# Four buffers for the decode's key pages, two of them placed in the row buffer that the input projection has finished reading

## The chip, the cores and the metric

The kernel runs on one core of a Trainium2 chip. The metric is the device time of one execution in microseconds; lower is better. The core has five engines that run their own instruction streams: TensorE (PE, matrix products), VectorE (DVE), ScalarE (ACT), GpSimd (POOL) and SyncE (SP). In this kernel SP and POOL issue nearly all DMAs in the stage that matters, and the transfers share 16 DMA engines.

## The reference, cut to what matters

One inference step of a two-layer decoder, for 256 prompt tokens and 8 sample (decode) tokens. Each layer projects its normalised input with `w_in` (1024 to 2048 columns) and mixes it in three ways; the part that matters is the attention of the 8 sample tokens over their cached keys and values, 256 positions in two pages of 128:

```python
def diff_attend(q, k, v, q_pos, k_pos, table, lam):
    s = jnp.einsum('bqhmd,bkhmd->bhmqk', q, k) * (DIFF_HEAD_DIM ** -0.5)
    s = s + rel_position_bias(q_pos, k_pos, table)[None, :, None]
    p = jax.nn.softmax(s, axis=-1)
    w = p[:, :, 0] - lam * p[:, :, 1]
    return jnp.einsum('bhqk,bkhe->bqhe', w, v)

k_past = cache_k[page_table, l]     # per sample: 2 pages x 128 positions x 512 numbers
v_past = cache_v[page_table, l]
```

After the mixers come the output projection `w_out` and a mixture of 64 experts (8 of them per token) with one shared expert. Six slices of `w_ada` times the conditioning vectors give the modulation of each layer.

## The kernel before, in words

All is float32. Activations lie transposed, features on the 128 partitions and the 264 tokens along the free axis: `hT` (8 x 264 columns) is the normalised input, `projT` the projected one. Semaphores order the engines by hand; a `Signal` counts per layer, and `by(layer, k)` is the k-th event of that layer. There are two layers, and each has the same stages.

*Projection.* TensorE makes 16 blocks of `w_in` times `hT` (line 1055) and signals `proj_made` after each. The weights come through `wide`, a pair of 2 MB buffers; SP fills them (line 614). A fill is two DMAs of 1 MB. Fill f = 5, the second with `w_ada`, waits for `proj_made` 16, the last block. Fills 6, 7 and 8 wait for the `ada` products 5, 6 and 7 of the layer in turn.

*Decode scores.* POOL loads pages with `load_k` and `load_v` (both through the helper on line 733), two DMAs of 256 KB for one sample. Keys go into `kbuf`, which has two buffers, values into `vbuf`, which has four. Samples 0 and 1 of the keys are loaded before the projection, the values of samples 0 to 3 when the last sine is made; the order on POOL's queue after that is this:

```python
for b in range(4):
    load_v(b)
for b in range(2, NS):
    pool.wait_ge(dec_products.sem, dec_products.by(layer, b - 1))
    load_k(b)
for b in range(4, NS):
    pool.wait_ge(dec_pv.sem, dec_pv.by(layer, b - 3))
    load_v(b)
```

For each sample b, TensorE copies its query row to all partitions (line 1122, into one of two PSUM banks, after the products of sample b - 2). VectorE multiplies it with the two key pages (line 1918, two instructions; the second signals `dec_products`) and sums over the features (line 1921). Between these TensorE has the two GLU products (line 1128, after sample 1) and the sixteen matmuls of `ada` (line 943, after the query of sample 4 and again after that of sample 7), and one turn of a modulation row (line 951). Then it waits for the last sum (`dec_scored`).

*Decode weights and values.* TensorE turns the scores (lines 903, 1140), VectorE and ScalarE make the softmax (lines 1930 to 1937), TensorE spreads the weights (lines 1145, 1146), and the values of samples 0 to 3 are multiplied (line 1153). Their `dec_pv` lets POOL load the values of samples 4 to 7. Behind them on POOL stand the stores of new keys, values and states (line 805).

*After that:* prompt attention with the remaining `ada` products, the output projection (line 1235), routing, the shared expert (line 1289), and then 96 expert steps. An expert step multiplies 64 gathered rows with the gate and up weights (line 1337) and with the down weights (line 1350); POOL gathers the rows into `xg` (line 842), and scatters the results (line 849). `hT` is written again by ScalarE with the squares of the second norm, after the first block of the output projection has been added.

Of the kernel before, what the change touches and what calls it, by code (L numbers as in the profile page):

```python
# [22 lines left out]
ALU = mybir.AluOpType  # L23
# [5 lines left out]
DEPTH = 2  # L29
NP_ = 256  # L30
NS = 8
# [9 lines left out]
PROJ = IN_W // P  # L41
# [5 lines left out]
PAGES = PAST // PAGE  # L47
# [152 lines left out]
def program(nc, a, out):  # L200
    ctx_list = []

    def keep(cm):
        ctx_list.append(cm)
        return cm.__enter__()
# [3 lines left out]
    def sb(name, shape, dt=F32):  # L209
        places[name] = -(-nc.sbuf_base // 32) * 32  # L210
        return keep(nc.sbuf_tensor(name, shape, dt))
# [5 lines left out]
    def sem(name):  # L217
        return keep(nc.semaphore(name))

    def sig(name, per_layer):  # L220
        return Signal(sem(name), per_layer)
# [4 lines left out]
    hT = sb("hT", [P, KD, T])  # L226
# [5 lines left out]
    kbuf = sb("kbuf", [P, 2, PAGES, 512])  # L232
# [50 lines left out]
    ps = keep(nc.psum_tensor("ps", [P, 8, 512], F32))  # L283
# [6 lines left out]
    ident = cst[:, K_ID:K_ID + P]  # L290
    ones = cst[:, K_ONE:K_ONE + P]
    half = cst[:, K_HALF:K_HALF + 2]

    xrows = projT[:, :, :].rearrange("p a b -> p (a b)")[:, 0:4 * D].rearrange("p (a b) -> p a b", a=4)
    skews = scratch[:, 0:HEADS * BUCKET_COLS].rearrange("p (h i) -> p h i", h=HEADS)
# [2 lines left out]
    prod = scratch[:, 0:1024].rearrange("p (g n) -> p g n", g=PAGES)  # L298
# [112 lines left out]
    proj_made = sig("proj_made", PROJ)  # L411
    proj_copied = sig("proj_copied", PROJ)
    rows_made, rows_out = sig("rows_made", 9), sig("rows_out", 9)
    k_loaded = [sig(f"k_loaded{n}", 16 * PAGES * NS // 2) for n in range(2)]
    v_loaded = [sig(f"v_loaded{n}", 16 * PAGES * NS // 4) for n in range(4)]
    q_spread = sig("q_spread", NS)
    dec_products = sig("dec_products", NS)
# [311 lines left out]
    def _(pool):  # L729
        gp = nc.gpsimd  # L730

        def load(sem_, dst, src):
            pool.dma_start(dst, src, allow_slow_non_contiguous=True).then_inc(sem_, 16)  # L733
# [22 lines left out]
        pages = [pool.value_load(pt[0:1, n:n + 1], min_val=0, max_val=kc.shape[0] - 1) for n in range(NS * PAGES)]  # L756
        kcf = kc.rearrange("n l t h d -> (n l) t (h d)")
        vcf = vc.rearrange("n l t h d -> (n l) t (h d)")
        pool.sem_inc(cache_stored, 1)
        for layer in range(DEPTH):  # L760

            def load_k(b):
                for g in range(PAGES):
                    load(k_loaded[b % 2].sem, kbuf[:, b % 2, g, :], kcf[pages[b * PAGES + g] * DEPTH + layer])

            def load_v(b):
                for g in range(PAGES):
                    load(v_loaded[b % 4].sem, vbuf[:, b % 4, g, :], vcf[pages[b * PAGES + g] * DEPTH + layer])
# [4 lines left out]
            for b in range(2):  # L773
                load_k(b)
# [17 lines left out]
            pool.wait_ge(sines_ready.sem, sines_ready.by(layer, 1 + SC // 2))  # L792
            for b in range(4):
                load_v(b)
            for b in range(2, NS):
                pool.wait_ge(dec_products.sem, dec_products.by(layer, b - 1))
                load_k(b)
            for b in range(4, NS):
                pool.wait_ge(dec_pv.sem, dec_pv.by(layer, b - 3))
# [35 lines left out]
            for t in range(3):  # L835
                n = P if t < 2 else NS
# [807 lines left out]
    def _(dve):  # L1644
        v = nc.vector
        ts, tt, stt, cp = v.tensor_scalar, v.tensor_tensor, v.scalar_tensor_tensor, v.tensor_copy
# [4 lines left out]
        for m in range(2):  # L1651
            ins = cp(relbs[:, :, :, m], relb[:, :].unsqueeze(1).to_broadcast([32, NS, HEADS]))
# [165 lines left out]
        for layer in range(DEPTH):  # L1818

            def W(s, k=1):  # L1820
                dve.wait_ge(s.sem, s.by(layer, k))
# [12 lines left out]
            for r in range(2):  # L1834
                for h in range(2):
                    src = ps[:, 6, 256 * r:256 * r + 256].rearrange("p (t k h c) -> p t k h c", t=2, k=4, h=2)[:, :, :, h, :]
                    dst = cT[:, r].rearrange("p t (k h c) -> p t k h c", k=4, h=2)[:, :, :, h, :]
                    for t in range(2):
                        ins = ts(dst[:, t], src[:, t], half[:, h:h + 1], -1.0 if r else 1.0, ALU.mult, ALU.mult)
# [64 lines left out]
            for c in range(2):  # L1904
                ins = stt(yv[:, c, :], projT[:, C_U + c, :], pT[:, R_SD + c:R_SD + c + 1], ps[:, 4 + c, 0:T], ALU.mult, ALU.add)
# [7 lines left out]
                ts(prodm[:, :, :, m], qk[:, :, :], half[:, m:m + 1], None, ALU.mult)  # L1913
            for b in range(NS):
                W(q_spread, b + 1)
                dve.wait_ge(k_loaded[b % 2].sem, k_loaded[b % 2].by(layer, 32 * (b // 2 + 1)))
                for g in range(PAGES):
                    ins = tt(prod[:, g, :], ps[:, 2 + b % 2, :], kbuf[:, b % 2, g, :], ALU.mult)
                ins.then_inc(dec_products.sem, 1)
                W(dec_products, b + 1)  # L1920
                ins = v.tensor_reduce(decS[:, :, 8 * b:8 * b + 8], prod.rearrange("p g (a d) -> p g a d", d=HD), AX.X, ALU.add)
                if b == NS - 1:
                    ins.then_inc(dec_scored.sem, 1)
                else:
                    chain(ins)
                if b == 3:
                    W(glu_gate)
                    tt(mixT[:, 6:8, :], zv, gv, ALU.mult).then_inc(ssm_mixed.sem, 1)
# [12 lines left out]
            for g in range(PAGES):  # L1941
                for b in range(NS):
                    ins = cp(w32[:, g, b, 4 * b:4 * b + 4], ps[:, 7, 32 * g + 4 * b:32 * g + 4 * b + 4])
# [32 lines left out]
            for h in range(HEADS):  # L1976
                ins = cp(oT[:, h, NP_:T], ps[:, 5, 32 * h:32 * h + 32].rearrange("p (b h) -> p h b", h=HEADS)[:, h, :])
# [25 lines left out]
            for c in range(KD):  # L2003
                W(out_made, c + 1)
                g = modT[:, 16 + c, :]
# [26 lines left out]
            for t in range(3):  # L2032
                for g in range(NG):
                    ins = v.max(g8[:, t, g, :], biased[:, t, PG * g:PG * g + PG])
# [4 lines left out]
            for t in range(3):  # L2039
# [3 lines left out]
                ins = tt(pairs2[:, t], other, me, ALU.is_equal)  # L2043
            chain(ins)
            for t in range(3):
                ins = tt(pairs2[:, t], pairs2[:, t], low, ALU.mult)
# [7 lines left out]
            for t in range(3):  # L2054
                ins = v.max(t8[:, t, :], masked[:, t, :])
            chain(ins)
            for t in range(3):
                ins = v.match_replace(masked[:, t, :], t8[:, t, :], masked[:, t, :], 3 * NEG)
# [24 lines left out]
            for t in range(3):  # L2083
                ins = v.max(t8[:, t, :], order[:, t, :])
# [7 lines left out]
            for t in range(3):  # L2092
                n = P if t < 2 else NS
# [71 lines left out]
            for k in range(TOPK):  # L2165
                for t in range(2):
                    W(y_loaded[k // 2], 32)
                    part, g = ypart[t][k // 2][:, k % 2, :], gk[:, t, k:k + 1]
# [52 lines left out]
```

## Time and profile before

| | us |
|---|---|
| median of 3 runs | 1956.47 |
| lowest and highest | 1954.2, 1957.7 |
| the profiled execution's own time | 1957.11 |
| its span | 1955.4 |
| TensorE busy | 1756.3 (90%) |
| VectorE busy | 670.0 (34%) |
| mean granted TensorE clock | 0.923 |

The span is counted from the first to the last instruction of the profiled execution; its own time holds 1.7 us more. A row of a timeline has its start in us, its duration in us, the engine, the source line, what is written and read, the count of instructions merged, and in brackets how long the engine stood idle before it and what released it.

### The profile page before, as it was taken

Reading aid. Unit: us, or ns where it says so; the run is one execution under the profiler, and the core shown is the slowest. Engines: PE = TensorE matmul, PEld = TensorE weight load, DVE = VectorE, ACT = ScalarE, POOL = GpSimd, SP = SyncE. Lnnn points to the kernel's source line nnn. Section 1 sums busy time; section 2 is a strip of 40 time slices with the busy share of each in tenths; the row PEclk is TensorE's granted clock in tenths of the full one; section 3 lists DMA queues with packets and bytes.
Section 4 is the critical chain, followed back from the end, with each engine's and each line's share of the span. In section 5 each row is a group of like instructions: output and inputs, shape, how many; then the busy total and the mean of one; then the engine's idle time right before and its main releaser. Section 6 shows DMA issues by size and latency. Waiting matters only on the chain.

```text
span 1955.4 us, 28143 instructions
## 1 busy us (share of the span) xinstructions
PE 1756.3 (90%) x11215; PEld 1004.8 (51%) x11215; DVE 670.0 (34%) x1678; ACT 341.3 (17%) x765; POOL 692.2 (35%) x754
## 2 busy tenths in 40 slices
PE   6996888999999999999589779788999999999974
PEld 3762466455555555555267337644555555555533
DVE  4773435322112322112469522541122112222216
ACT  3230311111112111111021221211111111111101
POOL 1214102445445455454012140053545445455420
PEclk9897688999999999999879778889999999999996
DMA  9457654998999999999934675579999999999943
GB/s 302 132 167 237 208 194 178 414 379 307 393 407 391 355 367 377 373 372 351 342 106 137 198 242 197 213 297 415 389 372 365 370 347 381 365 357 372 371 170 139
DMA packets 216639, 588.89 MB, mean 301 GB/s; under 512 B 67705, under 2 KB 147277, under 8 KB 162622
## 3 DMA queue, kind: packets, MB, share of 16 engines
q1 hardware_dynamic: 146224, 506.99, 67.9%
q0 software_dynamic: 67232, 79.73, 12.0%
q8 instruction: 90, 1.47, 0.3%
q10 hardware_dynamic: 3054, 0.38, 0.2%
q14 instruction: 39, 0.32, 0.0%
HBM read 775.22 MB, written 56.95 MB: 426 GB/s over the span
## 4 chain that ended last, share of the span: by engine, by line
PE 75%; DVE 8%; DMA 7%; issue 5%; SPq 2%; ACT 1%; another core or an unknown queue 1%; POOL 1%; POOLq 0%; ACTq 0%; DVEq 0%
PE ps L1337 34%; PE ps L1350 15%; PE ps L900 8%; PE ps L1055 4%; DMA xg<-hrows,idx_x 3%; PE ps L1235 3%; PE ps L943 2%; DMA ypart<-yrows_k 2%; PE ps L1289 1%; SPq L618 1%; PE ps L929 1%; DMA vbuf<-in_cache_v 1%; DMA raw<-in_w_ada 1%; PE ps L1266 1%
## 5 line engine op out<-in xcount | busy, mean ns | idle before, releaser
L1337 PE MATMUL ps<-raw,xTs 128*64 128x256 f32 x6144 | 745.4, 394 | 1.4 <-ACT xTs L1595 1.4
L1337 PEld LDWEIGHTS ps<-raw,xTs 128*64 128x64 f32 x6144 | 418.6, 135 | 268.8 <-issue 37.0
L849 POOL DMA_INDIRECT yrows_k<-ytok,idx_y x192 | 195.8, 1020 | 514.4 <-DVE ytok L2020 470.3
L1350 PE MATMUL ps<-dn,scratch 128*64 128x512 f32 x1536 | 363.6, 592 | 1.6 <-DVE scratch L2024 1.5
L2014 DVE TENSOR_TENSOR scratch<-scratch,ps 128x128 f32<-128x128 f32 x192 | 55.2, 288 | 750.6 <-ACT scratch L1617 662.1
L842 POOL DMA_INDIRECT xg<-hrows,idx_x x192 | 197.6, 1029 | 124.7 <-DVE idx_x L2108 66.5
L2020 DVE COPY ytok<-ps 128x512 f32<-128x512 f32 x192 | 132.7, 691 | 154.6 <-PE ps L1350 116.9
L1350 PEld LDWEIGHTS ps<-dn,scratch 128*64 128x64 f32 x1536 | 108.9, 135 | 146.9 <-issue 111.3
L1595 ACT ACTIVATE xTs<-ps 128x512 f32<-128x512 f32 x192 | 114.4, 597 | 382.3 <-PE ps L900 358.8
L900 PEld LDWEIGHTS ps<-cst,xg 128*128 128x128 f32 x768 | 81.7, 142 | 180.4 <-issue 146.3
L1617 ACT ACTIVATE scratch<-ps 128x128 f32<-128x128 f32 x192 | 53.2, 277 | 685.8 <-PE ps L1337 634.1
L900 PE MATMUL ps<-cst,xg 128*128 128x128 f32 x768 | 127.4, 289 | 28.4 <-DMA xg<-hrows,idx_x 26.8
L1055 PE MATMUL ps<-hT,wide 128*128 128x264 f32 x512 | 131.2, 418 | 9.5 <-DVE hT L1690 9.5
L1055 PEld LDWEIGHTS ps<-hT,wide 128*128 128x128 f32 x512 | 105.1, 208 | 30.1 <-issue 10.4
L900 PE MATMUL ps<-cst,scratch 128*128 128x128 f32 x224 | 63.4, 295 | 13.8 <-DVE scratch L1972 10.7
L855 POOL DMA_INDIRECT raw<-in_exp_w_up,idx_w x64 | 66.4, 1038 | 19.5 <-issue 19.2
L855 POOL DMA_INDIRECT dn<-in_exp_w_down,idx_w x64 | 65.1, 1017 | 22.6 <-issue 22.6
L2024 DVE COPY scratch<-ps 128x128 f32<-128x128 f32 x192 | 55.9, 291 | 49.5 <-PE ps L900 34.0
L855 POOL DMA_INDIRECT raw<-in_exp_w_gate,idx_w x64 | 63.8, 996 | 22.5 <-issue 19.0
L733 POOL DMA_DIRECT2D hrows<-htok x6 | 3.2, 539 | 188.9 <-ACT htok L1603 188.9
L733 POOL DMA_DIRECT2D vbuf<-in_cache_v x32 | 17.1, 539 | 116.3 <-ACT cosT L1459 74.2
L900 PE MATMUL ps<-cst,ysum 128*128 128x128 f32 x32 | 11.0, 447 | 51.5 <-DVE ysum L2173 51.5
(372 smaller groups left out, 1450.1 us busy)
## 6 DMA issues: line engine op xcount, KB each, us to landing
raw<-in_exp_w_gate SPq DMA_DIRECT2D x128, 1024.0 KB
raw<-in_exp_w_up SPq DMA_DIRECT2D x128, 1024.0 KB
dn<-in_exp_w_down SPq DMA_DIRECT2D x128, 1024.0 KB
wide<-in_w_ada SPq DMA_DIRECT2D x32, 1024.0 KB, 7.7
wide<-in_w_in SPq DMA_DIRECT2D x16, 1024.0 KB, 8.2
ypart<-yrows_k SPq DMA_DIRECT2D x16, 1024.0 KB, 11.9
raw<-in_w_ada SPq DMA_DIRECT2D x14, 1024.0 KB
kbuf<-in_cache_k POOLq DMA_DIRECT2D x32, 256.0 KB, 3.3
```

The costliest lines, as they stand in the source:

```text
L842: pool.indirect_dma_start(xg[n % NX][:, :], None, hrows.rearrange("t (h d) -> (t h) d", h=2), bass.IndirectOffsetOnAxis(ap=idx_x[:, b:b + ...
L849: pool.indirect_dma_start(yrows_k.rearrange("t (h d) -> (t h) d", h=2), bass.IndirectOffsetOnAxis(ap=idx_y[:, b:b + 1], axis=0), ytok[n % ...
L855: pool.indirect_dma_start(dst, None, a[name].rearrange(v, p=P), bass.IndirectOffsetOnAxis(ap=idx_w[:, o:o + 1], axis=0), bounds_check=P * ...
L900: return nc.tensor.transpose(dst, src, ident[0:n, 0:n])
L1055: ins = mm(ps[:, i % 2, 0:T], w[:, k, P * (i % 2):P * (i % 2) + P], hT[:, k, :], start=k == 0, stop=k == KD - 1)
L1235: ins = mm(ps[:, c % 4, 0:T], w[:, k, P * (c % 2):P * (c % 2) + P], mixT[:, k, :], start=k == out_order[0], stop=k == out_order[-1])
L1337: ins = mm(ps[64 * h:64 * h + 64, 2 + n % 2, 0:256], xTs[n % 2][:, k % 4, 64 * (k // 4):64 * (k // 4) + 64], w[:, k, h], start=k == 0, sto ...
L1350: ins = mm(ps[64 * h:64 * h + 64, 5 + n % 2, :], actT[:, n % 2, 64 * j:64 * j + 64], dn[n % NDOWN][:, j, 512 * h:512 * h + 512], start=j = ...
L1595: act_(xTs[n % 2][:, :, :].rearrange("p k r -> p (k r)"), ps[:, n % 2, :], ACT.Copy).then_inc(x_copied.sem, 1)
L2014: tt(act[:, n % 2, :], silu[:, n % 2, :], ps[:, 2 + n % 2, 128:256], ALU.mult).then_inc(act_ready.sem, 1)
L2020: cp(ytok[n % NY][:, :], ps[:, 5 + n % 2, :]).then_inc(y_copied.sem, 1)
L2024: cp(actT[:, n % 2, :], ps[:, 4, 0:P]).then_inc(actT_ready.sem, 1)
```

## The change

The decode's key pages get two more buffers, in the first 2 x 2 x 512 columns of `hT`. The buffer of sample b is now b mod 4. Keys of samples 2 and 3 wait for the last block of the input projection (which reads `hT`) and no longer for VectorE's products; those of samples 4 to 7 wait for the products that are four samples back.

```diff
+    kspare = hT[:, :, :].rearrange("p k t -> p (k t)")[:, 0:2 * PAGES * 512].rearrange("p (j g n) -> p j g n", j=2, g=PAGES)
+    kpages = [kbuf[:, 0], kbuf[:, 1], kspare[:, 0], kspare[:, 1]]
...
-    k_loaded = [sig(f"k_loaded{n}", 16 * PAGES * NS // 2) for n in range(2)]
+    k_loaded = [sig(f"k_loaded{n}", 16 * PAGES * NS // 4) for n in range(4)]
...
             def load_k(b):
                 for g in range(PAGES):
-                    load(k_loaded[b % 2].sem, kbuf[:, b % 2, g, :], kcf[pages[b * PAGES + g] * DEPTH + layer])
+                    load(k_loaded[b % 4].sem, kpages[b % 4][:, g, :], kcf[pages[b * PAGES + g] * DEPTH + layer])
...
             for b in range(4):
                 load_v(b)
-            for b in range(2, NS):
-                pool.wait_ge(dec_products.sem, dec_products.by(layer, b - 1))
+            pool.wait_ge(proj_made.sem, proj_made.by(layer, PROJ))
+            for b in range(2, 4):
+                load_k(b)
+            for b in range(4, NS):
+                pool.wait_ge(dec_products.sem, dec_products.by(layer, b - 3))
                 load_k(b)
...
             for b in range(NS):
                 W(q_spread, b + 1)
-                dve.wait_ge(k_loaded[b % 2].sem, k_loaded[b % 2].by(layer, 32 * (b // 2 + 1)))
+                dve.wait_ge(k_loaded[b % 4].sem, k_loaded[b % 4].by(layer, 32 * (b // 4 + 1)))
                 for g in range(PAGES):
-                    ins = tt(prod[:, g, :], ps[:, 2 + b % 2, :], kbuf[:, b % 2, g, :], ALU.mult)
+                    ins = tt(prod[:, g, :], ps[:, 2 + b % 2, :], kpages[b % 4][:, g, :], ALU.mult)
```

## Rows read from the trace of the kernel before

**Rows 1.** The page, chain that ended last, shares of the span by engine.

```profile
PE 75%; DVE 8%; DMA 7%; issue 5%; SPq 2%; ACT 1%; another core or an unknown queue 1%; POOL 1%; POOLq 0%; ACTq 0%; DVEq 0%
```

**Rows 2.** Timeline of VectorE, layer 0, decode scores.

```profile
147.17 1.29 DVE L1918 TENSOR_TENSOR scratch<-ps,kbuf 128x512 f32<-128x512 f32 x2 [1.32 <-PE ps L1122]
149.75 1.29 DVE L1918 TENSOR_TENSOR scratch<-ps,kbuf 128x512 f32<-128x512 f32 x2
...
156.95 1.22 DVE L1921 TENSOR_REDUCE decS<-scratch 128x16 f32<-128x1024 f32 x1
164.70 1.29 DVE L1918 TENSOR_TENSOR scratch<-ps,kbuf 128x512 f32<-128x512 f32 x2 [6.53 <-DMA kbuf<-in_cache_k]
```

**Rows 3.** Timeline of VectorE, layer 1, decode scores.

```profile
1108.52 1.29 DVE L1918 TENSOR_TENSOR scratch<-ps,kbuf 128x512 f32<-128x512 f32 x2 [5.26 <-DMA kbuf<-in_cache_k]
```

**Rows 4.** Timeline of TensorE, layer 0, decode scores to values.

```profile
158.97 3.64 PE L943 MATMUL ps<-wide,condT 128*32 128x512 f32 x16
162.54 1.26 PE L951 MATMUL ps<-cst,modrow_late 128*128 128x9 f32 x8
169.97 1.08 PE L903 MATMUL ps<-cst,decS 128*64 128x128 f32 x4 [6.17 <-DVE decS L1921]
...
176.33 3.67 PE L1153 MATMUL ps<-vbuf,w 128*32 128x512 f32 x16 [1.37 <-DVE w L1943]
```

**Rows 5.** Timeline of TensorE, layer 1, end of the scores.

```profile
1107.63 1.45 PE L951 MATMUL ps<-cst,modrow_late 128*128 128x9 f32 x8
1113.79 1.08 PE L903 MATMUL ps<-cst,decS 128*64 128x128 f32 x4 [4.71 <-DVE decS L1921]
```

**Rows 6.** Timeline of POOL, layer 0, page loads.

```profile
142.31 1.06 POOL L733 DMA_DIRECT2D kbuf<-in_cache_k  x2 [13.48 <-DVE scratch L1918]
...
149.11 1.13 POOL L733 DMA_DIRECT2D kbuf<-in_cache_k  x2 [3.16 <-DVE scratch L1918]
151.69 1.13 POOL L733 DMA_DIRECT2D kbuf<-in_cache_k  x2 [1.45 <-DVE scratch L1918]
154.88 1.13 POOL L733 DMA_DIRECT2D kbuf<-in_cache_k  x2 [2.07 <-DVE scratch L1918]
...
180.25 4.22 POOL L733 DMA_DIRECT2D vbuf<-in_cache_v  x8 [21.55 <-PE ps L1153]
```

**Rows 7.** Timeline of SP's queue, fills 5, 6 and 7 of layer 0.

```profile
134.88 0.99 SPq L614 DMA_DIRECT2D wide<-in_w_ada  x2
...
153.20 0.99 SPq L614 DMA_DIRECT2D wide<-in_w_ada  x2
...
162.67 0.99 SPq L614 DMA_DIRECT2D wide<-in_w_ada  x2
```

**Rows 8.** Time to landing: key pages issued 154.5 to 160, then `wide` 130 to 205.

```profile
DMA to landing us min/median/max: 6.6/7.7/9.1
...
DMA to landing us min/median/max: 5.2/8.1/17.1
```

**Rows 9.** Windows: start:end, length, busy of five engines, granted clock, DMA share, GB/s.

```profile
163.50:164.00 0.50, 0.30 (x3) 0.21 (x2) 0.00 (x0) 0.16 (x1) 0.00 (x0) 1.00 0.97 336
1109.00:1109.50 0.50, 0.09 (x1) 0.00 (x0) 0.50 (x2) 0.36 (x2) 0.00 (x0) 1.00 0.96 285
...
166.00:170.00 4.00, 0.03 (x1) 0.06 (x2) 3.73 (x4) 0.00 (x0) 0.00 (x0) 0.55 1.10 349
```

**Rows 10.** Timeline of TensorE: the same form of turn in two expert steps.

```profile
334.10 1.11 PE L900 MATMUL ps<-cst,xg 128*128 128x128 f32 x4 [5.91 <-DMA xg<-hrows,idx_x]
...
349.03 0.66 PE L900 MATMUL ps<-cst,xg 128*128 128x128 f32 x4
```

**Rows 11.** TensorE's waits in the expert steps, layer 0 then layer 1.

```profile
PE ps L900 <- DMA xg<-hrows,idx_x: 10.4, 2, 5.9
...
PE ps L900 <- DMA xg<-hrows,idx_x: 16.4, 4, 6.0
```

**Rows 12.** The chain that ended last, layer 0, one gather on POOL's queue.

```profile
364.73 20.02 DMA xg<-hrows,idx_x
```

## The prediction, as it was put on record before the change was run

> **What bounds the kernel now.** I read the page first: three quarters of the chain that ended last is TensorE [rows 1], most of it the expert steps, which this change doesn't touch. So the question is whether the two short decode stages, one for each layer, lie on the chain, and which wait ends last there. VectorE's timeline shows one long gap in each: before the products of sample 6 it waits 6.53 us in layer 0 [rows 2] and 5.26 us in layer 1 [rows 3], both times for the key pages' DMA. No other sample waits for a page. Then I asked whether anybody waits for VectorE. TensorE does: after its second `ada` product and a modulation turn it stands idle until the last sum is there, 6.17 us [rows 4] and 4.71 us [rows 5]. Behind it everything is a relay (softmax, weights, values, prompt attention), so an idle microsecond there is one of the run.
>
> Why sample 6 waits is seen on the two issuing queues. POOL issues its pages at 154.88 [rows 6], 1.7 us behind a 2 MB fill that SP issued at 153.20 [rows 7]. The four page DMAs of samples 6 and 7 took 6.6 to 9.1 us to land [rows 8]. DMAs issued at 151.69, ahead of that fill, were there when VectorE wanted sample 5: its sum started at 156.95, 1.3 us behind its products, without a wait [rows 2].
>
> **The change, part by part.** No arithmetic is added or removed. The same 16 page DMAs of each layer are issued by the same queue, with one wait exchanged; only their times move.
>
> *Samples 2 and 3.* Their wait is now `proj_made` 16. It fires when SP issues fill 5, at 134.88 [rows 7], while the first of these loads went out at 142.31 before [rows 6] and the other after the next products. POOL has nothing else to do then. One sample costs it about 1.06 us of issue, so the four DMAs leave from 134.9 to about 137.1, all behind a fill, and 3 MB are now in flight in place of 2. The nearest rows for pages behind a fill are those of samples 6 and 7, at most 9.1 us. Sample 2's last page leaves at 135.5 and is there by 144.6; it is wanted at 147.17, where VectorE waits for the query's matmul and not for a page [rows 2]. Sample 3's leaves at 136.6 to 137.1 and lands by 146.2; wanted at 149.75. Cost nothing, with 2.6 and 3.5 us to spare. The other end: 17.1 us, the longest landing of a fill [rows 8], or even the 20.02 us of a gather on POOL's queue [rows 12]; that is a rival below. The fill itself may land some 2 us later, but its `ada` product starts at 158.97 [rows 4], 24 us after the issue.
>
> *Samples 4 to 7.* Each now goes out when the sample before last once did. Sample 4 leaves at 142.31, sample 6 at 149.11 and sample 7 at 151.69 [rows 6], both before the fill of 153.20 [rows 7]. The loads that stood in these two slots before (samples 4 and 5) caused no wait. Sample 7 is not needed before about 160.8, 9.1 us after its issue starts, so even the worst landing of a page behind a fill would hold it by little.
>
> *What is late next on VectorE.* Sample 5's sum ends at 156.95 + 1.22 = 158.17 [rows 2]. The query of sample 6 was made long before; that of sample 7 is made right before 158.97 [rows 4]. So sample 6 starts at 158.2 in place of 164.70: 6.5 us. The step from one sample to the next is 149.75 - 147.17 = 2.58 us [rows 2], so the last sum ends at 158.2 + 5.16 = 163.4. In layer 1 the gap of 5.26 us closes to its last 0.04: 5.2 us.
>
> *What is late next on TensorE.* It is free of the modulation turn at 162.54 + 1.26 = 163.80 [rows 4], 0.3 us after the last sum would be seen. So TensorE itself takes over the bound, and the gain in layer 0 is its idle time, 6.17 us. In layer 1 it is free at 1107.63 + 1.45 = 1109.08 [rows 5], and the last sum would be there at about 1108.6: the gain is 4.71 us. Sum: 10.88 us. TensorE's work up to there keeps its times, since none of it waits for a page.
>
> *The clock of the turns.* The four turns of line 903 took 1.08 us at 169.97 [rows 4], where the granted clock was at the lower of its two levels (0.55 on average over 166 to 170, falling from the full one). In the new place, 163.80 and 1109.1, the granted clock was 1.00 in both layers [rows 9], and what TensorE does up to there is unchanged, so the clock should be as well. Four turns of 128 x 128 cost 1.11 us at the low level and 0.66 at the full one [rows 10]: 0.45 us for each layer, 0.9 in all. The bounds are 0 and 0.9; I take 0.9, as the windows are those of the very place.
>
> *Whether the rest moves along.* The values of samples 4 to 7 leave when the products of samples 0 to 3 end, before at 180.25 [rows 6], then at about 173.6. Fill 7 is issued at 162.67 [rows 7] and keeps that time, since it follows the `ada` product. It would land after 8.1 us, the median of these DMAs [rows 8], at 170.8, so 2.8 us ahead of the values. All other fills, stores and expert loads are released by TensorE's own events and shift with it. Fill 6 lands earlier, without the pages of samples 6 and 7 beside it. Cost nothing. The other end: if fill 7 took the longest landing, 17.1 us, it would run 6.2 us into the value loads; as two streams that share the engines end together, not one after the other, I price that case at 2.5 us for each layer, under half of the overlap.
>
> **Sum.** 6.17 + 4.71 + 0.9 = 11.8 us off the profiled execution's own 1957.11: 1945.3. The median of the runs is 0.64 us lower, 1956.47, so I predict 1944.7 us.
>
> **A rule of the skill, weighed.** During the idle time that goes away the granted clock fell from 1.00 to a mean of 0.55 [rows 9], and the 16 value matmuls after it took 3.67 us [rows 4] at the low level. The Trainium skill, "TensorE: Matmul & The Clock Gate", Part 1: The HAM clock gate, says that the throttled state is the default and that activity releases it, idle time brings it back. By that rule a TensorE that no longer idles could keep its full clock up to the values. The trace agrees that the clock falls in idle time. Whether the short turns and weights, some 2.4 us of matmuls in the 6 us between the last sum and the values, are enough, no row shows; by the rule the sum would be that of the second rival.
>
> **The rivals.** First, *the late pages behind fill 5*, which ends on the other side. Place: samples 2 and 3, at 147.17 and 149.75. For it: the pages now start with a fill, where the slow landings of before were. Against it: even the slowest of those, 9.1 us, is early enough. Were they to land like the gather, 20.02 us [rows 12], sample 3's would come at 157.1, 7.4 us late in each layer, and all behind it with them: 14.8 - 11.8 = 3 us slower, about 1959.5. It turns from gain to loss at a lateness of 5.9 us for each layer. At the 17.1 us of the slowest fill they are 4.4 us late: 1944.7 + 8.8 = 1953.5.
>
> Second, *the clock stays full to the values*: the 3.67 us at the low level [rows 4] would be half of it, about 1.8 less, the weights' matmuls some 0.5 shorter by the ratio of rows 10, 2.3 us for each layer, 4.6 in all: 1940.1. Against it: TensorE is idle more than half of that stretch, before and after.
>
> Third, *the value loads meet fill 7*, as priced above: 2 x 2.5 us, 1949.7. For it, 2.8 us is a thin margin; against it, fills 6 and 7 have less beside them than before.
>
> Fourth, *the expert steps start otherwise*. There TensorE waits for gathered rows, 10.4 us in layer 0 and 16.4 us in layer 1 [rows 11] for the same code. A shift against whatever paces the gathers could give layer 0 two more such waits or take them from layer 1: 6.0 us either way, 1938.7 or 1950.7. Against it: all that feeds these steps shifts together.
>
> Fifth, *the change does nothing*: the wait isn't on the path. Against it stands TensorE's own idle time of the same length.
>
> **How the numbers follow.** Forecast (within 2.5 us of 1944.7, the clock in the prompt attention being uneven): 0.65. Late pages 0.07, of which 0.03 slower. Full clock 0.08. Value loads 0.09. Expert steps 0.09, both ways together. Nothing 0.02. A measurement of this kernel tells about 0.2%, 3.9 us, from no change, so "faster" ends at 1952.6. Only the late pages at their mild price and the dead change end in between: same 0.05; slower 0.03; faster 0.92. The range of 8 in 10 runs from the lower expert case to the upper one: 1939 to 1950.
>
> **What the changed profile would show.** Right: two page loads of line 733 at 134.9 and 136; no idle time of VectorE before sample 6 for a DMA; its last sum ending near 163.3 and 1108.4 less the earlier shift of 6.6 us; before line 903 in either layer next to no idle time of TensorE, and the four turns at about 0.66 us; the distance from there to the output projection as before. Wrong: a wait for a page before sample 2, 3 or 7; a longer wait before the values of samples 4 to 7; or a sum of gather waits in the expert steps that isn't 10.4 and 16.4 us.

## The result, and the profile after

| | before | after |
|---|---|---|
| median, us | 1956.47 | 1945.45 |
| runs of the pair | 5 (1954.2 to 1958.94) | 5 (1943.05 to 1947.5) |
| ratio, 95% interval | | 0.9942 [0.9928, 0.9957] |
| profiled execution, span | 1957.11, 1955.4 | 1943.9, 1942.2 |
| mean granted TensorE clock | 0.923 | 0.924 |

The forecast was 1944.7 us, 11.8 us less; measured are 11.0 us between the medians and 13.2 between the two profiled executions. The whole interval of the ratio lies below 1: the changed kernel is 0.4 to 0.7% faster.

The views are those shown for the kernel before, now of the changed one (line numbers are 2 to 5 higher; line 1923 is the old 1918, 1926 the old 1921, 735 the old 733; in the experiments each row carries the line number of its own kernel, so the products are line 1920 there in experiments two and three). VectorE's timeline, layer 0, the answer to [rows 2]:

```profile
147.29 1.29 DVE L1923 TENSOR_TENSOR scratch<-ps,hT 128x512 f32<-128x512 f32 x2 [1.77 <-PE ps L1127]
149.87 1.29 DVE L1923 TENSOR_TENSOR scratch<-ps,hT 128x512 f32<-128x512 f32 x2
...
156.37 1.29 DVE L1923 TENSOR_TENSOR scratch<-ps,kbuf 128x512 f32<-128x512 f32 x2 [0.77 <-PE ps L1127]
157.69 1.22 DVE L1926 TENSOR_REDUCE decS<-scratch 128x16 f32<-128x1024 f32 x1
158.94 1.29 DVE L1923 TENSOR_TENSOR scratch<-ps,hT 128x512 f32<-128x512 f32 x2
...
162.84 1.22 DVE L1926 TENSOR_REDUCE decS<-scratch 128x16 f32<-128x1024 f32 x1
```

The gap of 6.53 us before sample 6 (at 158.94) is gone, and no row of VectorE waits for a page in either layer. In layer 1, the answer to [rows 3]:

```profile
1096.56 1.29 DVE L1923 TENSOR_TENSOR scratch<-ps,hT 128x512 f32<-128x512 f32 x2
...
1100.46 1.22 DVE L1926 TENSOR_REDUCE decS<-scratch 128x16 f32<-128x1024 f32 x1
```

TensorE's timeline of layer 0 and of layer 1, the answers to [rows 4] and [rows 5]:

```profile
154.21 5.58 PE L1127 MATMUL ps<-rowsS,oT 8*128 8x512 f32 x6
159.71 3.62 PE L948 MATMUL ps<-wide,condT 128*32 128x512 f32 x16
163.26 1.06 PE L956 MATMUL ps<-cst,modrow_late 128*128 128x9 f32 x8
164.25 0.65 PE L908 MATMUL ps<-cst,decS 128*64 128x128 f32 x4
...
170.12 3.55 PE L1158 MATMUL ps<-vbuf,w 128*32 128x512 f32 x16 [1.36 <-DVE w L1948]
...
177.71 1.90 PE L1158 MATMUL ps<-vbuf,w 128*32 128x512 f32 x4 [1.34 <-DMA vbuf<-in_cache_v]
182.92 5.96 PE L1158 MATMUL ps<-vbuf,w 128*32 128x512 f32 x12 [3.31 <-DMA vbuf<-in_cache_v]
...
1100.90 1.88 PE L956 MATMUL ps<-cst,modrow_late 128*128 128x9 f32 x8
1102.71 1.12 PE L908 MATMUL ps<-cst,decS 128*64 128x128 f32 x4
```

Neither turn of the scores (line 908) has a bracket any more: TensorE no longer stands idle before them. The queues, first POOL, layer 0 [rows 6]:

```profile
134.81 2.12 POOL L735 DMA_DIRECT2D hT<-in_cache_k  x4 [6.31 <-PE ps L1060]
142.34 1.13 POOL L735 DMA_DIRECT2D kbuf<-in_cache_k  x2 [5.40 <-DVE scratch L1923]
...
149.23 1.13 POOL L735 DMA_DIRECT2D hT<-in_cache_k  x2 [3.18 <-DVE scratch L1923]
151.80 1.13 POOL L735 DMA_DIRECT2D hT<-in_cache_k  x2 [1.44 <-DVE scratch L1923]
173.94 4.24 POOL L735 DMA_DIRECT2D vbuf<-in_cache_v  x8 [21.01 <-PE ps L1158]
```

and SP [rows 7]:

```profile
134.55 0.99 SPq L616 DMA_DIRECT2D wide<-in_w_ada  x2
...
154.34 1.00 SPq L616 DMA_DIRECT2D wide<-in_w_ada  x2
...
163.40 0.99 SPq L616 DMA_DIRECT2D wide<-in_w_ada  x2
```

Samples 6 and 7 leave at 149.23 and 151.80, ahead of the fill of 154.34. The time to landing of all the key pages issued in 130 to 160 (against [rows 8]) was:

```profile
DMA to landing us min/median/max: 2.8/3.5/6.9
```

Granted clock where the turns of the scores run (the number after POOL's busy time and count), layer 0 and layer 1, against [rows 9]; last the stretch of the queries of samples 5 to 7:

```profile
164.20:164.90 0.70, 0.70 (x8) 0.65 (x7) 0.00 (x0) 0.53 (x2) 0.00 (x0) 1.00 0.47 82
1102.70:1103.60 0.90, 0.90 (x5) 0.89 (x5) 0.00 (x0) 0.77 (x2) 0.00 (x0) 0.50 0.91 287
154.20:159.70 5.50, 5.50 (x10) 1.66 (x6) 4.63 (x7) 0.60 (x1) 0.00 (x0) 0.50 0.91 297
```

And the gathers of the expert steps in both layers, against [rows 11]:

```profile
PE ps L905 <- DMA xg<-hrows,idx_x: 11.1, 2, 6.0
...
PE ps L905 <- DMA xg<-hrows,idx_x: 16.2, 4, 6.1
```

### The profile page after: what moved, and what is told of

It is laid out like the page before. It is cut to its first block, busy times and chain, and to the rows that moved or that the text cites. A ratio compares the mean times of both kernels' runs of the same rounds, so it can differ in the third digit from the quotient of the medians.

```text
span 1942.2 us, 28143 instructions
## 1 busy us (share of the span) xinstructions
PE 1752.2 (90%) x11215; PEld 1002.3 (52%) x11215; DVE 669.8 (34%) x1678; ACT 342.4 (18%) x765; POOL 692.7 (36%) x754
## 4 chain that ended last, share of the span: by engine, by line
PE 75%; DVE 8%; DMA 7%; issue 5%; SPq 2%; ACT 1%; another core or an unknown queue 1%; POOL 1%; POOLq 0%; ACTq 0%; DVEq 0%
PE ps L1342 35%; PE ps L1355 16%; PE ps L905 8%; PE ps L1060 4%; DMA xg<-hrows,idx_x 3%; PE ps L1240 3%; PE ps L948 2%; DMA ypart<-yrows_k 2%; PE ps L1294 1%; SPq L620 1%; PE ps L934 1%; DMA raw<-in_w_ada 1%; DMA vbuf<-in_cache_v 1%; PE ps L1271 1%
## 5 line engine op out<-in xcount | busy, mean ns | idle before, releaser
L1342 PEld LDWEIGHTS ps<-raw,xTs 128*64 128x64 f32 x6144 | 419.9, 136 | 269.6 <-issue 39.1
L1060 PEld LDWEIGHTS ps<-hT,wide 128*128 128x128 f32 x512 | 102.9, 204 | 29.3 <-issue 10.4
L905 PE MATMUL ps<-cst,scratch 128*128 128x128 f32 x224 | 62.8, 292 | 16.2 <-DVE scratch L1977 13.1
L860 POOL DMA_INDIRECT raw<-in_exp_w_gate,idx_w x64 | 63.8, 997 | 22.3 <-issue 18.7
## 6 DMA issues: line engine op xcount, KB each, us to landing
raw<-in_w_ada SPq DMA_DIRECT2D x14, 1024.0 KB, 10.6
```

The lines of the kernel that those rows point to most:

```text
L860: pool.indirect_dma_start(dst, None, a[name].rearrange(v, p=P), bass.IndirectOffsetOnAxis(ap=idx_w[:, o:o + 1], axis=0), bounds_check=P * ...
L905: return nc.tensor.transpose(dst, src, ident[0:n, 0:n])
L1060: ins = mm(ps[:, i % 2, 0:T], w[:, k, P * (i % 2):P * (i % 2) + P], hT[:, k, :], start=k == 0, stop=k == KD - 1)
L1342: ins = mm(ps[64 * h:64 * h + 64, 2 + n % 2, 0:256], xTs[n % 2][:, k % 4, 64 * (k // 4):64 * (k // 4) + 64], w[:, k, h], start=k == 0, sto ...
```

## The experiments

Each was timed beside the kernel before on its own chip, so ratios are compared and not microseconds. The theory: pages of samples 6 and 7 were late because they ran beside a 2 MB fill, and TensorE's idle time behind them was on the path.

**One. Samples 6 and 7 late again.**

```diff
-                pool.wait_ge(dec_products.sem, dec_products.by(layer, b - 3))
+                pool.wait_ge(dec_products.sem, dec_products.by(layer, b - 3 if b < 6 else b - 1))
```

> The changed kernel, but the key pages of samples 6 and 7 wait again for the products they waited for before (sample 5's and 6's, one and two samples back), samples 2 to 5 as changed. Theory: all of the gain comes from samples 6 and 7 leaving ahead of the 2 MB fill. Then VectorE waits 5 to 7 us for a page before sample 6 in both layers again, TensorE 4 to 6 us before the turns of the scores, and the time is that of the kernel before, 1956 +- 2 us. Rival: the gain comes from samples 2 and 3 being there early, or from four buffers as such. Then it stays at 1945.5 +- 2.

Measured: 0.9999 [0.9985, 1.0013]. The whole gain is gone although four buffers and the early samples 2 and 3 stay. VectorE's and TensorE's rows, and the landing of the pages issued from 153 on:

```profile
160.60 1.29 DVE L1923 TENSOR_TENSOR scratch<-ps,hT 128x512 f32<-128x512 f32 x2 [4.02 <-DMA hT<-in_cache_k]
```

```profile
165.87 1.09 PE L908 MATMUL ps<-cst,decS 128*64 128x128 f32 x4 [3.04 <-DVE decS L1926]
```

```profile
DMA to landing us min/median/max: 5.7/6.1/6.5
```

The wait before sample 6 is smaller than the one I expected (4.02 us in layer 0 and 4.17 in layer 1, not 5 to 7; 8.2 us in all against 11.8 before), and TensorE's idle time is 6.9 us in all against 10.9. By that this kernel should have been 4 us, 0.2%, faster than the one before; the interval just misses it. The profiled execution (1942.71 us) is the fastest of its ten, so it may not stand for the others; the difference isn't settled.

**Two. Samples 2 and 3 late, 4 to 7 as changed.**

```diff
-            pool.wait_ge(proj_made.sem, proj_made.by(layer, PROJ))
-            for b in range(2, 4):
-                load_k(b)
-            for b in range(4, NS):
-                pool.wait_ge(dec_products.sem, dec_products.by(layer, b - 3))
+            for b in range(2, NS):
+                pool.wait_ge(dec_products.sem, dec_products.by(layer, b - 1 if b < 4 else b - 3))
                 load_k(b)
```

> The changed kernel, but the key pages of samples 2 and 3 wait for the first and second products as they did before, in their new buffers; samples 4 to 7 as changed, so that on POOL's queue samples 4 and 5 leave right behind 3. Theory: 1945.5 +- 2, no wait of VectorE for a page, since only the issue of samples 6 and 7 ahead of the fill counts; sample 4 and 5 leave about 1 us apart after sample 3. Rival, the early issue of samples 2 and 3 carries the gain: 1950 to 1956, with a wait before sample 2, 3 or 4.

Measured: 0.9942 [0.9921, 0.9962], as the change. The issue of samples 2 and 3 beside fill 5 bought nothing, and cost nothing, that the time can show. Eight DMAs went out between 140 and 146, and VectorE waited for no page:

```profile
140.21 1.06 POOL L735 DMA_DIRECT2D hT<-in_cache_k  x2 [13.48 <-DVE scratch L1920]
142.79 1.06 POOL L735 DMA_DIRECT2D hT<-in_cache_k  x2 [1.52 <-DVE scratch L1920]
143.91 2.33 POOL L735 DMA_DIRECT2D kbuf<-in_cache_k  x4
147.38 1.13 POOL L735 DMA_DIRECT2D hT<-in_cache_k  x2 [1.15 <-DVE scratch L1920]
```

**Three. No new buffer; the fill waits instead.** On the kernel before:

```diff
             wait_wide(layer, f)
+            if f == WIDE_IN + 2:
+                sp.wait_ge(dec_products.sem, dec_products.by(layer, NS))
             for j in range(2):
```

> The kernel before with its two key buffers, but SP holds fill 6 until the products of sample 7 are made. Theory, the fill is what makes the pages of samples 6 and 7 late: they land in about 3 us in place of 7 to 9, VectorE waits under 0.6 us before sample 6, TensorE's idle time before the turns is under 1 us, and the time is 1945 to 1947. Fill 6 and 7 then leave together at about 163 and 164; the ada product at 173 could wait 0 to 3 us for fill 6, which would add up to 6 us. Rival, the pages are late because two buffers leave too little time whatever else runs: 1956, with the wait of 5 to 7 us unchanged.

Measured: 0.9947 [0.9927, 0.9967]. The pages leave as late as in the kernel before (153.97 and 156.86), but without a fill beside them:

```profile
DMA to landing us min/median/max: 2.9/3.0/3.1
```

```profile
154.92 1.29 DVE L1920 TENSOR_TENSOR scratch<-ps,kbuf 128x512 f32<-128x512 f32 x2 [0.35 <-DMA kbuf<-in_cache_k]
...
157.78 1.29 DVE L1920 TENSOR_TENSOR scratch<-ps,kbuf 128x512 f32<-128x512 f32 x2 [0.31 <-DMA kbuf<-in_cache_k]
```

3.0 us to landing in place of 6.6 to 9.1 [rows 8], for the same DMAs at the same point of the stage: the cause is shown to be the fill beside them, not the number of buffers. The rows above are samples 5 and 6. With two buffers VectorE still waits 0.3 us for each of samples 5 to 7 in layer 0, and 0.5 us once in layer 1. No `ada` product waited for its fill.

**Four. Both cures together**, the change and the held fill, first in four executions and then, beside the changed kernel itself, in six.

> The changed kernel, and SP holds fill 6 until the products of sample 7 are made, as in the experiment on the kernel before. Theory: both edits cure one cause, the pages of samples 6 and 7 beside the fill, so they don't add up: ratio 0.9945 +- 0.001 to the kernel before, as the change alone (0.9942) and the held fill alone (0.9947). Rival, each took away a delay of its own: 0.989.

Measured: 0.9906 [0.987, 0.9943], executions from 1932.81 to 1946.77 us: too wide to decide. So it was repeated:

> The changed kernel as it is, beside the next run on the same chip. Expected: its ratio of 0.9942 to the kernel before, within 0.0015. Its executions should scatter by some 10 us, as those of the other kernels did; where the prompt attention runs is where I expect the scatter: 43 to 46 us for that stage in most profiles, 39 in two, with the same instructions.

> The changed kernel with fill 6 held until the products of sample 7 are made, again, since its first interval (0.987 to 0.9943) held both theories. One cause: the same ratio as the changed kernel beside it, within 0.0015, some 0.9945. Two causes: 0.989.

Measured: the changed kernel 0.9937 [0.9917, 0.9956], both cures 0.9943 [0.9921, 0.9964]. 0.989 lies outside both of these intervals: the two cures don't add up, as is to be expected of one cause. The executions of the changed kernel lay from 1937.64 to 1944.84 us, those with both cures from 1936.17 to 1946.63.

**Five. The modulation turn after the turns of the scores**, to test that TensorE itself became the bound. Diff: in TensorE's stream

```diff
-            W(glu_gate)
-            ada_turn(layer, ADA_FIRST, 4, 256)
             W(st_copied)
...
                start=True, stop=True).then_inc(dec_turned.sem, 1)
+            W(glu_gate)
+            ada_turn(layer, ADA_FIRST, 4, 256)
```

and in ScalarE's `ada_columns(ADA_FIRST, 4, 256)` from ahead of the exponential to behind it.

> The changed kernel, and the modulation turn that TensorE makes after its second ada product of the layer moves behind the turns of the scores (ScalarE's copy of it behind the exponential). Theory, TensorE itself is the bound in layer 1 of the changed kernel: there the last sum of VectorE ended at 1101.68 and the turns of the scores began at 1102.71, when TensorE was free. They should now begin within 0.2 us of the last sum in both layers, which is 0.9 us earlier in layer 1 and nothing in layer 0, where VectorE was already the later one; the moved 1 to 1.9 us hide in the 2.5 us in which TensorE waits for the softmax. 1 us is less than a time can show, so only the trace is read. Rival: the moved turn delays the weights by what it takes and nothing is gained.

The rows of layer 1, first VectorE's last sum, then TensorE:

```profile
1104.98 1.22 DVE L1926 TENSOR_REDUCE decS<-scratch 128x16 f32<-128x1024 f32 x1
```

```profile
1106.35 1.09 PE L908 MATMUL ps<-cst,decS 128*64 128x128 f32 x4 [0.86 <-DVE decS L1926]
```

The turns now begin at 1106.35, 0.15 us after the sum's end at 1106.20; in the changed kernel it was 1102.71 - 1101.68 = 1.03 us. So TensorE was the bound there by 0.9 us. In layer 0 they begin at 164.72, also 0.15 us behind the last sum. The rival failed: from the turns to the spreading of the weights it is 3.22 and 3.73 us, in the changed kernel 3.25 and 3.76. One run, 1944.57 us, says nothing on the time.

**Six. The value pages in the key buffers.** The next wait in this stage is the one for the values of samples 4 to 7. The changed kernel has four key buffers that come free at 154 to 163 and stay empty until the experts' weights or the second norm use their place:

```diff
-                    load(v_loaded[b % 4].sem, vbuf[:, b % 4, g, :], vcf[pages[b * PAGES + g] * DEPTH + layer])
+                    load(v_loaded[b % 4].sem, (vbuf[:, b] if b < 4 else kpages[b % 4])[:, g, :], vcf[pages[b * PAGES + g] * DEPTH + layer])
...
             for b in range(4, NS):
-                pool.wait_ge(dec_pv.sem, dec_pv.by(layer, b - 3))
+                pool.wait_ge(v_loaded[b % 4].sem, v_loaded[b % 4].by(layer, 32))
+                pool.wait_ge(dec_products.sem, dec_products.by(layer, b + 1))
                 load_v(b)
...
-                    ins = mm(ps[32 * j:32 * j + 32, 5, :], w32[:, g, b, :], vbuf[:, j, g, :], start=b < 4 and g == 0,
+                    ins = mm(ps[32 * j:32 * j + 32, 5, :], w32[:, g, b, :], (vbuf[:, b] if b < 4 else kpages[j])[:, g, :], start=b < 4 and g == 0,
```

> The changed kernel, and the value pages of samples 4 to 7 go into the four key buffers as the key products free them (after the products of samples 4 to 7), in place of the value buffers of samples 0 to 3 after their matmuls. In the changed kernel TensorE's values of samples 4 to 7 take from 176.4, when the turn before them ends, to 188.8, with waits for pages between; without waits they would take 3.7 us. Theory: 8.7 us less in layer 0 and 8.4 in layer 1, 1928 +- 3 us. Rival: the eight pages now meet fills 6 and 7, a later ada product waits for its fill, and half of it is given back: 1937.

Measured: 0.9836 [0.9797, 0.9875], with experiment seven the fastest kernel of this study; 1.1% below the changed one. The rival failed, though by little: one weight load of an `ada` product is put down to its fill (0.84 us, at 179.36), but TensorE's matmuls ran on without idle time. TensorE, layer 0, the 16 matmuls of samples 4 to 7 and what follows:

```profile
176.52 0.63 PE L1159 MATMUL ps<-kbuf,w 128*32 128x512 f32 x2
176.55 0.63 PE L1159 MATMUL ps<-hT,w 128*32 128x512 f32 x2
...
177.86 0.60 PE L1159 MATMUL ps<-hT,w 128*32 128x512 f32 x2
178.40 1.04 PE L1169 MATMUL ps<-rowsS,wself 8*32 8x512 f32 x2
```

From the first value matmul to the one of the new token it takes 178.40 - 170.27 = 8.1 us (changed kernel: 188.81 - 170.12 = 18.7), in layer 1 8.3 in place of 18.3. I had expected 8.7 and 8.4 us less; it is 10.6 and 10.0. Nearly all of the difference is the clock: my sum took the 16 matmuls at the 3.7 us of the low level, and they took 1.9 us at a granted clock of 1.00.

**Seven. Five and six together.**

> The kernel of the values experiment (value pages of samples 4 to 7 in the key buffers) with the modulation turn moved as well. Theory: 0 to 2 us below the values kernel, whose ratio to the kernel before was 0.9836, so 0.982 to 0.984 here. Rival: 0.985 or more, if the later copy of the modulation delays the exponential or the next product.

Measured: 0.9845 [0.9826, 0.9864]: not told apart from six, as the 1 us at stake can't be.

## Why the prediction was right

*Both gaps on the path.* Right. The stage between SP's fill 5 and the turns of the scores shrank from 169.97 - 134.88 = 35.09 to 164.25 - 134.55 = 29.70 us in layer 0, by 5.39 (forecast 6.17), and in layer 1 from 1113.79 - 1080.10 = 33.69 to 1102.71 - 1073.38 = 29.33, by 4.36 (forecast 4.71). Experiments one and three show the cause from both sides.

*TensorE takes over the bound.* Right, but in layer 0 at a later time than I forecast. In layer 1 experiment five shows it. In layer 0 VectorE's last sum ended at 164.06. By the 0.15 us of experiment five it could have let the turns go at 164.21; they began at 164.25, back to back with the modulation turn, so the two engines were late together. Both were behind the forecast after the 0.33 us by which the execution was ahead: VectorE by 1.0 us, and TensorE by 164.25 - 163.47 = 0.78 us, which is all that is missing between 6.17 and 5.39. The rows put this down to the clock. TensorE shows no idle time from 145.1 to 163.2 and was granted the low level throughout (the kernel before had 0.91 over its queries, 145.9 to 150.1):

```profile
145.10:163.20 18.10, 18.10 (x45) 4.50 (x44) 15.22 (x20) 1.45 (x3) 3.04 (x6) 0.50 0.68 222
```

The six matmuls of the queries of samples 5 to 7 took 5.58 us, and sample 5 waited 0.77 us for its query; sample 2 waited 1.77 us for its own, 1.32 before. "TensorE's work up to there keeps its times" is the sentence that was too strong: no page delays it, but the granted clock fell elsewhere.

*The turns at the full clock*, 0.9 us. Half right: 0.65 us at a clock of 1.00 in layer 0, and 1.12 at 0.50 in layer 1, where the modulation turn ahead of them was slow too (1.88 for 1.45). I had taken the clock of a place in one execution for a property of the place. The window that I read in layer 1 also lay behind TensorE's work, when it already stood idle; over the modulation turn itself, 1107.6 to 1109.1, the kernel before had 0.71.

So the terms came to 5.39 + 4.36 + 0.5 = 10.2 us in place of 11.8 (0.5 is what the turns saved up to VectorE's next instruction, all of it in layer 0), close to the 11.0 between the medians. The profiled executions differ by 3 us more, in stretches that the change doesn't touch. Layer 1's prompt attention, from the turn of the decode's output to the first matmul of the output projection, was 1.0 us shorter (44.7 and 43.7 us), layer 0's 0.7 us longer (43.0 and 43.7); 1.5 us lie between there and fill 5 of layer 1, and 1.0 behind layer 1's prompt attention. I take that for scatter, as below; no run separates it from an effect of the change.

That the sum came out so close is in part luck. The second profile of the same kernel (experiment four) has 165.75 - 138.06 = 27.69 us from fill 5 to the turns in layer 0 and 1103.55 - 1074.68 = 28.87 in layer 1, 7.40 and 4.82 less than before, and both turns at the full clock (0.62 and 0.65 us). In layer 0 even the two GLU products ahead of the scores, the same instructions, differ by 1.7 us, here in the kernel before and in that second profile:

```profile
142.30 3.72 PE L1128 MATMUL ps<-scratch,gluw 128*128 128x264 f32 x8 [0.76 <-ACT scratch L1525]
```

```profile
145.48 2.05 PE L1133 MATMUL ps<-scratch,gluw 128*128 128x264 f32 x8 [0.75 <-ACT scratch L1530]
```

So one term of this sum moves by 2 us between two executions of one kernel.

*Samples 2 and 3 beside fill 5.* Right: at most 6.9 us to landing in layer 0 and 8.0 in layer 1, bounded at 9.1. Sample 2 started at 147.29 behind its query. Experiment two shows that they could have stayed late as well.

*The value loads and fill 7.* Right: 18.7 and 18.3 us from the first value matmul to that of the new token against 18.4 and 18.4 before. *The clock stays full to the values*: no; 3.55 us for 3.67. TensorE's long idle time was gone (2.54 and 1.36 us of idle time remain between the turns and the values), and the granted clock was 0.57 on average over 170 to 174 all the same. Here the rule of the Trainium skill ("TensorE: Matmul & The Clock Gate", Part 1), that activity releases the throttled state, was no guide: the trace has 18.1 us at 0.50 without idle time (above). *The expert steps*: 11.1 and 16.2 us of gather waits, forecast 10.4 and 16.4.

## What to carry to other kernels

A page load that takes three times as long as its neighbours tells of what was issued just ahead of it: put the issue times of all queues side by side before adding a buffer, since an earlier issue and a later bulk fill cure the same wait, and not twice. When a wait is gone, price the next one on each engine, down to the microsecond at which the other engine takes over. And once there are more buffers, ask which other loads could use them while they stand empty: here that was worth almost twice the change.

## What the runs showed that was not expected

*Column groups.* The values of samples 4 to 7 go into four column groups of 32. In the changed kernel sample 4's four matmuls took 1.90 us, alone because their pages came alone (177.71 above). With all pages there, the 16 matmuls of the four samples ran in 178.4 - 176.5 = 1.9 us together, at the same granted clock of 1.00. A late page costs here not only its wait but the company of the other groups. In layer 0 of the changed kernel TensorE waited 1.34 + 3.31 = 4.7 us for these pages and multiplied for 1.90 + 5.9 = 7.8 us, the last 5.9 at a granted clock of 0.71 on average; with all pages there it was 1.9 us and no wait. So of the 10.6 us that experiment six gained there, more than half is not waiting. No run varies the company alone.

*The clock in the prompt attention.* The same instructions took 43.0 to 45.4 us in this stage in most profiles and 39.2 and 39.1 in layer 1 of experiments three and five. Windows over it, the changed kernel and then the other two:

```profile
1131.10:1174.80 43.70, 34.44 (x182) 16.96 (x181) 17.66 (x60) 17.58 (x59) 3.37 (x7) 0.71 0.67 218
```

```profile
1124.90:1164.10 39.20, 29.56 (x183) 15.11 (x182) 17.67 (x60) 17.57 (x59) 4.76 (x10) 0.84 0.77 244
```

```profile
1134.10:1173.20 39.10, 29.46 (x182) 14.97 (x182) 17.68 (x60) 17.56 (x59) 4.18 (x9) 0.84 0.77 246
```

VectorE's and ScalarE's busy times are equal; TensorE's is 29.5 us in place of 34.4, and the granted clock 0.84 in place of 0.71. So 4 to 5 us of the scatter between executions can come from this stage of one layer alone. What decides it was not tested.
